# Context keys and values as a chunk of their own in a two-block transformer kernel, with the last four steps by token block

## What is computed

```python
y = (gelu(gate) * val) @ w_down          # end of the first block, K = 5632
x = x + rmsnorm(y, post_ffn_g)
h = modulate(rms_norm(x, norm_attn_w_2), shift, scale)        # 256 tokens
hc = modulate(rms_norm(ctx_2, norm_attn_w_2), shift_c, scale_c)  # 256 context tokens
q, k, v, u = split(h @ w_in_2)           # 2048 x 2560: q 1024, k 256, v 256, u 1024
k_ctx, v_ctx = hc @ w_in_2[:, 1024:1536] # the 512 columns of k and v
```

## Time and profile before

| | |
|---|---|
| median of 3 runs | 2201.51 us (2199.18 to 2206.2) |
| the profiled execution | 2204.18 us, its span 2202.5 us |
| TensorE busy | 2162.4 us, 98% |
| VectorE, ScalarE busy | 1521.8 us (69%), 1078.5 us (49%) |
| steps of 12 matmuls, junction | 2.72 us each |

### The profile page before, as it was taken

How to read it: one execution, slowest core, us unless ns; L and a number is a source line. 1 busy time by engine, 2 the same in 40 slices (tenths; PEclk the granted TensorE clock), 3 DMA queues, 4 the chain that set the end, 5 groups by cost and what they waited for, 6 DMA issues and landing times.

```text
span 2202.5 us, 32471 instructions
## 1 busy us (share of the span) xinstructions
PE 2162.4 (98%) x10304; PEld 1790.4 (81%) x10304; DVE 1521.8 (69%) x1895; ACT 1078.5 (49%) x1449; POOL 133.0 (6%) x233
## 2 busy tenths in 40 slices
PE   8999999999999999999999999999999999999998
PEld 7888888888778888788887778888888888888876
DVE  7997679788997878768776354566545655555656
ACT  6445654655434554345577355464434434434433
POOL 2110001100000001100000000000000000000000
PEclk9999899999999999999999999999999999999999
DMA  9887077788888888977755251557656666766652
GB/s 333 291 269 244 2 259 238 254 276 280 260 286 273 271 279 269 313 230 241 240 166 179 93 170 41 169 167 266 217 193 229 222 196 210 239 194 212 221 175 101
DMA packets 277678, 482.85 MB, mean 219 GB/s; under 512 B 25997, under 2 KB 118485, under 8 KB 276257
## 3 DMA queue, kind: packets, MB, share of 16 engines
q1 hardware_dynamic: 247168, 367.22, 50.1%
q0 software_dynamic: 30192, 113.72, 16.4%
q10 hardware_dynamic: 176, 0.08, 0.0%
HBM read 478.81 MB, written 2.11 MB: 218 GB/s over the span
## 4 chain that ended last, share of the span: by engine, by line
PE 94%; ACT 2%; DVE 2%; issue 1%; DMA 0%; POOL 0%; ACTq 0%; POOLq 0%; DVEq 0%
PE G L1775 28%; PE G L1777 28%; PE G L1776 28%; PE T L2043 2%; PE T L2158 1%; PE T L1964 1%; PE G L1944 1%; PE T L1809 1%; ACT w_hi L583 1%; PE G L2138 1%; PE T L1989 0%; ACT junk L529 0%; PE T L1990 0%; PE T L1991 0%; PE G L1872 0%
## 5 line engine op out<-in xcount | busy, mean ns | idle before, releaser
L1057 DVE TENSOR_TENSOR w_lo<-raw,w_hi 128x1024 fp32r<-128x1024 f32 x696 | 840.0, 1217 | 457.1 <-ACT w_hi L583 454.7
L583 ACT ACTIVATE w_hi<-raw 128x1024 fp32r<-128x1024 f32 x696 | 732.9, 1055 | 839.5 <-PE G L1777 834.9
L1775 PE MATMUL G<-w_hi,h_hi 128*128 128x512 f32 (+1 forms) x1904 | 746.5, 392 | 4.7 <-ACT p L606 2.4
L1777 PE MATMUL G<-w_hi,h_lo 128*128 128x512 f32 (+1 forms) x1904 | 739.6, 388 | 0.0
L1776 PE MATMUL G<-w_lo,h_hi 128*128 128x512 f32 (+1 forms) x1904 | 738.9, 388 | 0.0
L1775 PEld LDWEIGHTS G<-w_hi,h_hi 128*128 128x128 f32 x1904 | 358.2, 188 | 77.9 <-issue 4.2
L1777 PEld LDWEIGHTS G<-w_hi,h_lo 128*128 128x128 f32 x1904 | 357.8, 188 | 73.9
L1776 PEld LDWEIGHTS G<-w_lo,h_hi 128*128 128x128 f32 x1904 | 358.2, 188 | 70.7
L1775 PE MATMUL G<-w_hi,a_hi 128*128 128x512 f32 x880 | 346.3, 393 | 8.4 <-issue 5.6
L1777 PE MATMUL G<-w_hi,a_lo 128*128 128x512 f32 x880 | 343.5, 390 | 0.0
L1776 PE MATMUL G<-w_lo,a_hi 128*128 128x512 f32 x880 | 343.3, 390 | 0.0
(11 more groups left out here) (275 smaller groups left out, 1225.2 us busy)
## 6 DMA issues: line engine op xcount, KB each, us to landing
ada_w<-in_w_ada POOLq DMA_DIRECT2D x192, 512.0 KB, 4.7
raw<-in_w_up SPq DMA_DIRECT2D x352, 256.0 KB, 4.3
raw<-in_w_mlp_up SPq DMA_DIRECT2D x256, 256.0 KB, 2.8
raw<-in_w_mlp_down SPq DMA_DIRECT2D x256, 256.0 KB, 3.4
...
raw<-in_w_out SPq DMA_DIRECT2D x128, 256.0 KB, 3.9
...
```

The costliest lines, as they stand in the source:

```text
L583: act.activation(w_hi[:, s % 4, :, 0:width], raw[:, s % 8, :, 0:width], ACT.Copy).then_inc(hi_ready, 1)
L1057: dve.tensor_tensor(w_lo[:, s % 4, :, 0:width], raw[:, s % 8, :, 0:width], w_hi[:, s % 4, :, 0:width].bitcast(F32), ALU.subtract).then_inc ...
L1775: pe.matmul(out, ah, wh, start=f, stop=False)
L1777: mm = pe.matmul(out, al, wh, start=False, stop=l)
```

## The change

The context's keys and values become a chunk of their own, the first of `in2`, on parity 0 from `h_hi`, `h_lo`; the five chunks of the tokens follow from `a_hi`, `a_lo`, on alternating parities. K2's columns are therefore loaded and split twice, and `in2` has 6 chunks. The buffers that shared the regions "h" and "act" change places. The context's squares, root and scalings move one chunk earlier, to chunks 1 and 2 of `down1c`. From the last steps of `down1c` to the end of the first chunk of tokens, the orders of TensorE, ScalarE and VectorE are written out call by call: the context's turns and steps stand where the identity's transposes and the waits stood. `keep_busy(84, 0)` is gone. The cross product's unread output goes to `u_buf` or PSUM. `last_steps` takes a number of steps, and waits for each step's weights inside block 0's loop. At the very end it orders four steps, and each block has its own root, scalings and output. The rest of the diff renames the buffers in later calls and renumbers the semaphores' counts.

```diff
--- before.py
+++ after.py
...
-          ("up1c", 6, 4), ("down1c", 4, 3), ("in2", 5, 4), ("out2", 4, 4), ("mlp2", 32, 4)]
+          ("up1c", 6, 4), ("down1c", 4, 3), ("in2", 6, 4), ("out2", 4, 4), ("mlp2", 32, 4)]
...
     FIRST_LOAD[_name], FIRST_EVAC[_name] = _l, _e
     _l += _n * _per
+    _e += 2 * _n
 LOADS = _l
...
-    vx2 = place("vx2", [P, 2 * NB, KV2, PV], "act", 24 * KB_)
+    vx2 = place("vx2", [P, 2 * NB, KV2, PV], "h", 24 * KB_)
...
-        for k, col in enumerate((0, N, K2, U2, U2 + N)):
+        for k, col in enumerate((K2, 0, N, K2, U2, U2 + N)):
...
-        pool.wait_ge(h_ready, PREP["ctx"] + UNITS)
+        pool.wait_ge(h_ready, PREP["in2"] + UNITS)
...
-            if q >= 2:
+            if q >= 2 or name == "in2":
...
@@ -839,33 +839,31 @@
             if c == 1:
                 his(s + 3, 3)
                 y_squares(0)
-                his(s + 6, 3)
+                act.wait_ge(ctx_in, 16)
+                hi(s + 6)
+                ctx_squares(0)
+                hi(s + 7)
+                ctx_squares(1)
+                hi(s + 8)
+                ctx_squares(2)
             elif c == 2:
-                act.wait_ge(ctx_in, 16)
                 hi(s + 3)
-                ctx_squares(0)
+                ctx_squares(3)
                 hi(s + 4)
-                ctx_squares(1)
+                root("ctx")
                 hi(s + 5)
                 y_squares(1)
-                hi(s + 6)
-                ctx_squares(2)
-                hi(s + 7)
-                ctx_squares(3)
-                hi(s + 8)
-            else:
-                hi(s + 3)
-                root("ctx")
-                hi(s + 4)
                 act.wait_ge(rstd_ready, STAT["ctx"] + 1)
                 for q in range(4):
                     ctx_scale(q)
-                hi(s + 5)
-                y_squares(2)
                 hi(s + 6)
                 for q in range(4, UNITS):
                     ctx_scale(q)
                 hi(s + 7)
+                hi(s + 8)
+
+        def ctx_high(q):
+            high_shifted("ctx", q, combc, adac[:, 6, :], h_hi)
 
         tile = 0
...
-            for c in range(1, 4):
+            for c in range(1, 3 if n == 6 else 4):
...
+        def y2_squares(b):
+
+            act.wait_ge(bank_evac, FIRST_EVAC["in2"] - 1 + b)
+            square(y[:, b, 3 * N:4 * N], sq[:, b, 3:4])
+            act.wait_ge(crossed, 4 + b)
+            square(u_buf[:, b, :], dots[:, 0, b, 3:4])
...
+        hi(s0 - 3)
+        ctx_high(0)
+        hi(s0 - 2)
+        ctx_high(1)
+        hi(s0 - 1)
+        y_squares(2)
+        hi(s0)
+        hi(s0 + 1)
+        ctx_high(2)
+        hi(s0 + 2)
+        hi(s0 + 3)
+        y2_squares(0)
+        ctx_high(3)
+        y2_squares(1)
+        hi(s0 + 4)
+        root("y2")
+        ctx_high(4)
+        root("in2")
+        hi(s0 + 5)
+        hi(s0 + 6)
+        ctx_high(5)
+        ctx_high(6)
+        hi(s0 + 7)
+        act.wait_ge(rstd_ready, STAT["in2"] + 1)
+        in2_scale(0)
+        hi(s0 + 8)
+        ctx_high(7)
+        in2_scale(1)
+        hi(s0 + 9)
+        in2_high(0)
+        in2_scale(2)
+        hi(s0 + 10)
+        in2_high(1)
+        hi(s0 + 11)
+        in2_scale(3)
+        in2_high(2)
+        hi(s0 + 12)
+        in2_scale(4)
+        in2_high(3)
+        in2_scale(5)
+        in2_high(4)
+        hi(s0 + 13)
+        in2_scale(6)
+        hi(s0 + 14)
+        in2_high(5)
+        in2_scale(7)
+        evac(lambda b: c2[:, b, :], 0, s=s0 + 8)
+        hi(s0 + 15)
+        in2_high(6)
+        hi(s0 + 16)
+        in2_high(7)
+        hi(s0 + 17)
+        hi(s0 + 18)
...
-            link(dve.tensor_tensor_reduce(out=conv[:, 0:2, :].rearrange("p a b -> p (a b)"), in0=z, in1=x[:, b, c * N:c * N + N],
+            link(dve.tensor_tensor_reduce(out=G[:, 2 + b, :] if c == 3 else u_buf[:, 0, :], in0=z, in1=x[:, b, c * N:c * N + N],
...
                 combine(combc, NORM_A, 7)
                 los(s + 7, 2)
             elif c == 2:
-                los(s + 3, 3)
-                times_row(1)
+                lo(s + 3)
                 dve.wait_ge(g_turned, 1)
                 dve.tensor_copy(grow[:], T[0:16, 3, 0:P]).then_inc(g_copied, 1)
-                los(s + 6, 3)
-            else:
-                lo(s + 3)
+                lo(s + 4)
                 root("ctx", rstdc[:], sums=sqc)
-                los(s + 4, 2)
-                times_row(2)
+                lo(s + 5)
+                for q in range(4):
+                    ctx_scale(q)
+                times_row(1)
                 lo(s + 6)
-                for q in range(UNITS):
+                for q in range(4, UNITS):
                     ctx_scale(q)
-                lo(s + 7)
+                los(s + 7, 2)
+
+        def ctx_low(q):
+            low_shifted("ctx", q, h_hi, h_lo)
 
         ctx_scale = scale_rows(cx, cx, lambda q, b: rstdc[:, b:b + 1])
...
-        root("y2", rstd[:, 0:NB])
-        dve.wait_ge(squared, SQUARED["in2"])
-        dve.wait_ge(root_ready, STAT["in2"] + 1)
-        dve.reciprocal(rstdx[:], ssq[:, 4:4 + NB]).then_inc(rstd_ready, 1)
-        dve.wait_ge(rstd_ready, STAT["in2"] + 1)
...
+        def y2_mean():
+
+            link(dve.tensor_reduce(ssq[:, 0:NB], sq[:], AX_X, ALU.add))
+            dve.tensor_scalar(ssq[:, 0:NB], ssq[:, 0:NB], 1.0 / D, EPS, ALU.mult, ALU.add).then_inc(mean_ready, 1)
...
+        def y2_root():
+            r = rstd[:, 0:NB]
+            dve.wait_ge(root_ready, STAT["y2"] + 1)
+            dve.reciprocal(r, ssq[:, 4:4 + NB]).then_inc(rstd_ready, 1)
+            dve.wait_ge(rstd_ready, STAT["y2"] + 1)
+            dve.wait_ge(squared, SQUARED["in2"])
+            link(dve.tensor_reduce(sums[:], dots[:].rearrange("p k b c -> p (k b) c"), AX_X, ALU.add))
...
+        def in2_root():
+            dve.wait_ge(root_ready, STAT["in2"] + 1)
+            dve.reciprocal(rstdx[:], ssq[:, 4:4 + NB]).then_inc(rstd_ready, 1)
+            dve.wait_ge(rstd_ready, STAT["in2"] + 1)
...
-        begin(2 * FIRST_LOAD["in2"], in2_rows, lambda q: low_shifted("in2", q, h_hi, h_lo))
+        s0 = 2 * FIRST_LOAD["in2"]
+        lo(s0 - 3)
+        ctx_low(0)
+        lo(s0 - 2)
+        down_evac(2, s0 - 6)
+        lo(s0 - 1)
+        ctx_low(1)
+        times_row(2)
+        lo(s0)
+        lo(s0 + 1)
+        y2_sum(0)
+        lo(s0 + 2)
+        lo(s0 + 3)
+        y2_sum(1)
+        ctx_low(2)
+        y2_mean()
+        ctx_low(3)
+        y2_root()
+        lo(s0 + 4)
+        ctx_low(4)
+        lo(s0 + 5)
+        lo(s0 + 6)
+        in2_root()
+        ctx_low(5)
+        in2_rows(0)
+        ctx_low(6)
+        in2_rows(1)
+        lo(s0 + 7)
+        lo(s0 + 8)
+        in2_rows(2)
+        lo(s0 + 9)
+        ctx_low(7)
+        in2_rows(3)
+        in2_low(0)
+        lo(s0 + 10)
+        in2_rows(4)
+        in2_low(1)
+        lo(s0 + 11)
+        in2_rows(5)
+        in2_low(2)
+        lo(s0 + 12)
+        in2_rows(6)
+        in2_low(3)
+        in2_rows(7)
+        lo(s0 + 13)
+        lo(s0 + 14)
+        in2_low(4)
+        in2_low(5)
+        lo(s0 + 15)
+        in2_low(6)
+        lo(s0 + 16)
+        in2_low(7)
+        lo(s0 + 17)
+        lo(s0 + 18)
...
+        los(s0 + 19, 17)
...
-        root("final", rstdx[:])
         for b in range(NB):
+            cols = slice(3 * N, 4 * N)
+            if b == 0:
+                dve.wait_ge(block_done, 4)
+            else:
+                dve.wait_ge(step_done, STEPS)
+            weighed(3, b)
+            dve.wait_ge(bank_evac, FIRST_EVAC["mlp2"] + 16 * GROUPS2 - 1 + b)
+            dve.tensor_tensor(x[:, b, cols], x[:, b, cols], y[:, b, cols], ALU.add).then_inc(x_new, 1)
+            dve.wait_ge(x_new, X_NEW["final"] + 3 + b + 1)
+            weighed_out(cols, slice(b, b + 1))
+            root(f"final_{b}", rstdx[:, b:b + 1], at=b, blocks=slice(b, b + 1))
...
-        def last_steps(s, acts, kt, ready):
-
-            for k in range(2):
-                pe.wait_ge(hi_ready, s + k + 1)
-                pe.wait_ge(lo_ready, s + k + 1)
-                pe.wait_ge(*ready(kt // STEPK + k))
+        def last_steps(s, acts, kt, ready, n=2):
+
             for b in range(NB):
-                for k in range(2):
+                for k in range(n):
+                    if b == 0:
+                        pe.wait_ge(hi_ready, s + k + 1)
+                        pe.wait_ge(lo_ready, s + k + 1)
...
-            for c in range(4):
-                steps(sd + per * c, 2 if c == 0 else 0, 4 if n == 6 and c == 3 else per, c % 2, A, ready, ed + 2 * (c - 1), per=per,
+            for c in range(3 if n == 6 else 4):
+                steps(sd + per * c, 2 if c == 0 else 0, per, c % 2, A, ready, ed + 2 * (c - 1), per=per,
                       fold=FOLD_DOWN.get((g, c), ()))
-                if n == 6 and c == 3:
-                    last_steps(sd + 22, A[0], 8, ready)
                 if c == 1 and g == "c":
                     pe.wait_ge(ada_col, 6)
```

(120 more changed lines are left out.)

103 lines of the change are left out of this document (44 added, 59 removed).

## The result

The kernel after takes 2185.51 us, the median of 4 runs (2182.20 to 2189.57); the kernel before beside it takes 2200.82 (2199.18 to 2206.20). The ratio is 0.9923 [0.9906, 0.9941], which is 15.3 us less (the interval is 13 to 21). 2184.0 and 17.5 us less were forecast. Executions of one kernel differ by several microseconds far ahead of the change: from TensorE's wait near 212 to the one near 377, after's profiled execution takes 164.57 us and e8's 159.82, with 0.88 and 0.93 as the granted clock over 200 to 300; before's has 164.61 and 0.88, so before's and after's traces are a fair pair.

The account below looks back on a forecast made before the run. TensorE, busy for 98% of the span, was taken as the bound. Junction 14.9 us less (16.7 - 1.8) plus end 2.6 gave 17.5 off the before median 2201.51: 2184.0 us, range 2179 to 2193 (likeliest case 2179 to 2188).

Parts of the forecast that it names:

- Useful work and its surplus: Old junction, last down steps to first scores: 175.07 us, 158.4 of it useful steps and turns, 16.7 removable.
- The waits of the new order: New junction, queues walked: 1.2 us of placed waits plus 0.6 of restarts, 1.8 in all.
- s0-6, `w_lo`: First down step after the context's turns: its weights, hanging on the context's landing, 0.5 us in hand or 0.2 late.
- `ctx_low(2)`: Early context step: low half made behind block 1's sum of squares on VectorE, TensorE waits 0.1 to 0.2 us.
- `ctx_low(7)`: Last context step: low half ready at 1165.3 behind other VectorE work, step due at 1165.1, a wait of 0.3 us.
- s0+36, rotation: Start of chunk U2: VectorE rotates block 0 before the fifth step's weights; 0.26 + 1.3 - 1.0, a 0.6 us wait.
- The cover: Junction: K2's second load and split (4 MB, 16 DMAs, 8 `hi`, 8 `lo`) stays hidden and adds nothing on TensorE.
- The end: Behind the last matmul: block 0 finishes early, block 1 has two scalings and two DMAs; 2.6 us less.
- The slip of the lockstep: Rival, 17%: in the junction's 16 units TensorE loses about half a microsecond each; 4 to 9 us lost, 2188 to 2193.
- The roots: Rival, 7%: roots and sums each stop TensorE 2 to 3 us; 10 to 16 us gone, 2194 to 2200.
- The clock: Rival, 3%: junction steps fall to the 1.2 GHz level, up to 2.72 us more each; seven eat the gain, twelve give 2217.
- The late context: Rival, 1%: context lands late in the junction; each microsecond beyond 0.5 costs one, 18 undo everything.

Follow-up runs that it names:

- e8: The kernel after run again unchanged, beside the one with three moves: 0.9924 of the kernel before, 2184.52 us.
- e7: The kernel after with three moves on VectorE and ScalarE that make the late-arriving data of three TensorE waits earlier: 0.9913 of before, 2182.39 us.
- e4: The kernel after with the 84 identity transposes put back between the last down step and the first context turn: 0.9961 of before.
- e2: The kernel after with the old end put back (two steps by block, one root), so the new junction alone: 0.9929 of before.
- e5: The kernel after with the context's load held back by a POOL memset of its buffer (3.53 us): 0.9927 of before, median 2186.24 us.
- e1: The kernel before with only the new end (last four steps by block, root and output per block): 0.9984 of before, 2200.12 us.
- e3: The kernel before without its 84 identity transposes, nothing else changed: 0.9994 of before.

## Why the prediction was right

**Useful work and its surplus.** 158.4 was counted from the price of a step and of a turn. e7 shows 158.31, and 158.05 without its one wait of 0.26. The surplus of 16.7 in the old junction was therefore right within 0.4 (175.07 - 158.05 = 17.0), and e4 shows that its largest term, the transposes, is paid (9.15 of 9.33) once no wait covers it. The lower bound was not worked out right: had the removed 12.6 us come back as waits, 4.1 of the 16.7 would have been left, not nothing.

**The waits of the new order**, 1.8 forecast. After shows 159.88 - 158.05 = 1.83, by place (time lost, against the pitch of a step or e8's start of s0-6):

| place | forecast | after | other runs |
|---|---|---|---|
| s0-6, `w_lo` | 0.5 in hand, or 0.2 late | 0.17 | 0.74 (e2), 0.49 (e4), none (e8) |
| `ctx_low(2)` | 0.1 to 0.2 | 0.48 | 0.45 (e2, e8) |
| `ctx_low(7)` | 0.3 | none | 0.26 (e7) |
| s0+36, rotation | 0.6 | 0.91 | 0.90 to 0.91 (e2, e4, e5, e8) |
| restarts and hand-overs | 0.6 | about 0.3, the rest | |

All four places are real. e7 removes three of them by moving just what was named, and brings out the fourth, `ctx_low(7)`, which after hides. The walk added the delays of `ctx_low(2)` and `ctx_low(7)`, 0.1 to 0.2 and 0.3; in fact TensorE waits at the first one it comes to, for 0.48 in after, and the wait there covers the second. The sum of the two was right, the split was not. The sum of 1.8 is right in part by luck: the rotation was 0.3 too cheap, and the allowance for restarts 0.3 too dear. No row of before showed that wait at its new size. Half of the 0.3 is in the first term of 0.26 + 1.3 - 1.0: it is the idle time at 1263.35, while the time lost there, over the pitch, is 0.41. The load of the queues was set too low: over 1126.6 to 1192.9 VectorE is busy for 58.0 and ScalarE for 60.1, against some 54 and 55 in the walk.

**The cover.** The 16 further DMAs, `hi` and `lo` cost TensorE nothing: with DMA at 195 GB/s no wait in the junction is put down to a DMA of `raw`.

**The end.** 2.6 forecast, 2.67 measured (2.6 in e1). The pieces fit as well: 3.4 for a DMA that finds one ahead of it was the one guess in it, and the slowest takes 3.4.

**Rivals.** The slip of the lockstep (half a microsecond a unit) didn't come: from 1153 to 1193 no unit of after waits. The roots don't stop TensorE. The clock stays at 1.00 through the junction; but it is nearer than 3% made it look, since e5 shows that one gap of 2.31 is enough to lower it. It is also cheaper than the rival had it: 1.6 in e5, 1.4 in e3, not a dozen steps at the lower level. The late context was sized by a rule, each microsecond beyond 0.5 costs one, that names the wrong step. By the prediction's own prices s0-12's weights were some 2 us ahead (landing, `hi` and `lo` end at 1106.5, wanted at 1108.4); e8 and e5 put it at 1.5, and a delay is caught there first. Once TensorE has stood there, s0-6 has its slack back.

**What wasn't forecast** is the 1.95 and 1.31 us outside the junction and the end. On the scale of the profiled execution it explains all of 2189.57 against 2186.7: 2.9 = 1.95 + 1.31 - 0.3 (junction) - 0.1 (end). In the medians the distance is smaller, 2185.51 against 2184.0, but with four executions of each kernel, which spread over 7 us in both groups, a hit within 1.5 us is luck in part. The prediction set the stretch between the first scores and the last four steps at no change; the seven traces with the new junction have 0.1 to 1.5 us more there than the three with the old one. What causes the wait in the MLP, and where the waits between 548 and 892 come from, was not tried.
